# Forward token transforms in three rounded passes in place of one fp32 pass, in a two-layer GLA and Hyena encoder

## The reference, cut to what matters

```python
h = rmsnorm(x, norm_mix)
q, k, v, r, g_lr, hy_in = split(h @ w_in)
x = x + concat([gla_group(q, k, v, r, g_lr), hyena_group(hy_in)]) @ w_out
x = x + (silu(h2 @ w_gate) * (h2 @ w_up)) @ w_down        # h2 = rmsnorm(x, norm_ffn)

def fft_long_conv(u, k_freq, d):            # u: (B, 256, 512)
    y = irfft(rfft(u, n=512, axis=1) * k_freq, n=512, axis=1)[:, :256]
    return y + u * d

def hyena_group(u, ...):
    v, x1, x2 = split(short_conv_centred(u))
    k_freq = hyena_filters(...)             # sin-FFN(positions) @ w3, times exp(-t * deltas)
    z = x1 * fft_long_conv(v, k_freq[:, 0], skip[0])
    z = x2 * fft_long_conv(z, k_freq[:, 1], skip[1])
    return rmsnorm(z, norm_w)
```

## Time and profile before

| | us |
|---|---|
| median of 3 runs (lowest, highest) | 1272.35 (1271.86, 1273.59) |
| the profiled execution, device time | 1274.18 |
| its span in the profile | 1272.4 |
| TensorE busy | 1232.2 (97%) |
| VectorE busy | 712.2 (56%) |
| ScalarE busy | 683.5 (54%) |
| GpSimd busy | 674.1 (53%) |
| a unit's load of 512 KB, issue to landing, median | 3.5 |

### The profile page before, as it was taken

One profiled execution on the slowest core, in us unless ns is written; L12 is line 12 of the kernel. 1 busy time (PEld: TensorE's weight loads), 2 busy tenths in 40 slices (PEclk: granted clock), 3 DMA queues, 4 the chain that ended last, 5 costly groups with the idle time before them and its releaser, 6 DMA issues.

```text
span 1272.4 us, 23307 instructions
## 1 busy us (share of the span) xinstructions
PE 1232.2 (97%) x9196; PEld 1068.6 (84%) x9196; DVE 712.2 (56%) x1117; ACT 683.5 (54%) x1340; POOL 674.1 (53%) x483
## 2 busy tenths in 40 slices
PE   5989999999999999999999999999999999999997
PEld 4656877879999999988877777778899999998885
DVE  5865766667677777400057475674877776760003
ACT  5756664547665555422256765654576655653223
POOL 2565672566465354566636666428364433346661
PEclk9999999999999999999999999999999999999999
DMA  5211112140423323233322212123223323323222
GB/s 220 95 50 59 60 51 84 50 165 25 140 93 115 119 77 106 101 99 99 99 67 78 72 52 67 36 82 126 74 84 100 100 100 108 120 89 107 94 98 82
DMA packets 31211, 115.96 MB, mean 91 GB/s; under 512 B 3456, under 2 KB 3712, under 8 KB 30720
## 3 DMA queue, kind: packets, MB, share of 16 engines
q1 hardware_dynamic: 31104, 114.49, 26.6%
HBM read 112.37 MB, written 2.10 MB: 90 GB/s over the span
## 4 chain that ended last, share of the span: by engine, by line
PE 82%; DVE 8%; ACT 4%; issue 3%; POOL 1%; DMA 1%; SPq 0%; POOLq 0%; DVEq 0%; ACTq 0%
PE ps L1941 10%; PE ps L1944 10%; PE ps L1943 10%; PE ps L1805 6%; PE ps L1827 6%; PE ps L1825 6%; PE ps L1824 6%; PE ps L1807 6%; PE ps L1806 6%; PE ps L2084 2%; PE ps L2098 2%; PE ps L1821 2%; PE ps L1816 2%; PE ps L1818 2%; POOL w_lo L1141 1%
## 5 line engine op out<-in xcount | busy, mean ns | idle before, releaser
L1141 POOL TENSOR_TENSOR w_lo<-w_raw,w_hi 128x1024 fp32r<-128x1024 f32 x108 | 266.2, 2466 | 303.1 <-ACT w_hi L671 229.8
L671 ACT ACTIVATE w_hi<-w_raw 128x1024 fp32r<-128x1024 f32 x108 | 113.9, 1055 | 187.5 <-PE ps L1827 171.1
L1941 PE MATMUL ps<-h_hi,w_hi 128*128 128x256 f32 x672 | 191.0, 284 | 0.0
L1943 PE MATMUL ps<-h_lo,w_hi 128*128 128x256 f32 x672 | 190.1, 283 | 0.0
L1944 PE MATMUL ps<-h_hi,w_lo 128*128 128x256 f32 x672 | 190.1, 283 | 0.0
L1805 PE MATMUL ps<-h_hi,w_hi 128*128 128x512 f32 (+1 forms) x392 | 166.0, 423 | 3.8 <-POOL w_lo L1141 1.1
L1941 PE MATMUL ps<-sum_hi,w_hi 128*128 128x256 f32 x528 | 150.2, 284 | 3.6 <-DVE silu L1366 2.2
L1807 PE MATMUL ps<-h_hi,w_lo 128*128 128x512 f32 (+1 forms) x392 | 152.8, 390 | 0.0
L1806 PE MATMUL ps<-h_lo,w_hi 128*128 128x512 f32 (+1 forms) x392 | 152.2, 388 | 0.0
L1943 PE MATMUL ps<-sum_lo,w_hi 128*128 128x256 f32 x528 | 149.4, 283 | 0.0
L1944 PE MATMUL ps<-sum_hi,w_lo 128*128 128x256 f32 x528 | 149.3, 283 | 0.0
(11 more groups left out here) (269 smaller groups left out, 2824.7 us busy)
## 6 DMA issues: line engine op xcount, KB each, us to landing
w_raw<-in_units SPq DMA_DIRECT2D x110, 512.0 KB, 3.5
u<-in_pairs SPq DMA_DIRECT2D x44, 512.0 KB, 3.9
w_raw<-in_pairs SPq DMA_DIRECT2D x40, 512.0 KB, 4.0
gain<-in_gain SPq DMA_DIRECT2D x5, 512.0 KB, 4.3
par<-in_par SPq DMA_DIRECT2D x2, 1214.5 KB, 8.8
x<-in_x SPq DMA_DIRECT2D x4, 512.0 KB, 7.3
spec<-in_pairs SPq DMA_DIRECT2D x4, 512.0 KB, 5.0
out_y<-x SPq DMA_DIRECT2D x4, 512.0 KB, 2.6
```

The source lines that it names most:

```text
L671: nc.scalar.activation(w_tile(g, 0), w_raw[:, g % RAW], ACT.Copy).then_inc(s_hi, 1)
L1141: nc.gpsimd.tensor_tensor(w_tile(g, 1), w_raw[:, g % RAW], w_tile(g, 0).bitcast(F32), ALU.subtract).then_inc(s_lo, 1)
L1941: nc.tensor.matmul(out, hi[:, cols], factor[m][0][:, k], start=start and k == 0, stop=False, skip_group_check=True)
L1943: nc.tensor.matmul(out, hi[:, cols], factor[m][1][:, k], start=False, stop=False, skip_group_check=True)
```

## The change

Each token tile is now kept as `u_hi` (rounded by ACT) and `u_lo` (DVE, PSUM minus `u_hi`), and the table as `dft_hi` (ACT) and `dft_lo` (POOL). `spectrum` makes three `float32r` matmuls where there was one of float32. Everything that waited for `utc` before it used the tiles, or banks 6 and 7, now waits for `utl`, the count of the DVE subtractions. `dft_hi` and `dft_lo` stand where the decay window is, and `u_lo` where the last filter weights are, so the window is loaded anew once (512 KB) behind unit 29's load in layer 0, and DVE waits for that load before it makes the filters of layer 1.

```diff
-C_MISC = C_Z + P
+C_MISC = (C_Z + P + 7) // 8 * 8
@@ build: tiles
-        u_tok = sb("u_tok", 2 * HY, at=xs_at)[:, :].rearrange("p (t c) -> p t c", t=2)
+        u_hi = sb("u_hi", 2 * HY, F32R, at=xs_at)[:, :].rearrange("p (t c) -> p t c", t=2)
+        u_lo = sb("u_lo", 2 * HY, F32R, at=par_at + 4 * C_W3)[:, :].rearrange("p (t c) -> p t c", t=2)
+        dft_hi = sb("dft_hi", 4 * P, F32R, at=cst_at + 4 * K_WIN)[:, :].rearrange("p (f e c) -> p f e c", f=2, e=2)
+        dft_lo = sb("dft_lo", 4 * P, F32R, at=cst_at + 4 * K_WIN + 16 * P)[:, :].rearrange("p (f e c) -> p f e c", f=2, e=2)
@@ sync, behind load_unit
+                    if L + 1 < DEPTH and n == U_OUT + 4:
+                        sp.wait_ge(ufp.sem, ufp.at(L, 8))
+                        sp.dma_start(cst[:, K_WIN:N_CST], cst_d[:, K_WIN:N_CST]).then_inc(s_decay, 16)
@@ scalar, turn_copy
-                    nc.scalar.activation(u_tok[:, t], ps[:, 6 + t, :], ACT.Copy).then_inc(utc.sem, 1)
+                    nc.scalar.activation(u_hi[:, t], ps[:, 6 + t, :], ACT.Copy).then_inc(utc.sem, 1)
@@ scalar, slots, behind hi_unit and factors
+                    if slot == 9:
+
+                        act.wait_ge(abr.sem, abr.at(L, 4))
+                        nc.scalar.activation(dft_hi, dft, ACT.Copy).then_inc(s_dft_hi, 1)
@@ gpsimd, slots, behind lo_unit
+                    if slot == 9:
+                        pool.wait_ge(s_dft_hi, L + 1)
+                        nc.gpsimd.tensor_tensor(dft_lo, dft, dft_hi.bitcast(F32), ALU.subtract).then_inc(s_dft_lo, 1)
@@ vector
+            def token_rests(L, i):
+                for t in range(2):
+                    v.wait_ge(utc.sem, utc.at(L, 2 * i + t + 1))
+                    nc.vector.tensor_tensor(u_lo[:, t], ps[:, 6 + t, :], u_hi[:, t].bitcast(F32), ALU.subtract)\
+                        .then_inc(utl.sem, 1)
@@ vector, slots, near the start
+                    if (slot - 1, 1) in T_AT:
+                        token_rests(L, T_AT[slot - 1, 1])
                     if (slot - 1, 1) in D_AT:
                         spectrum_halves(L, D_AT[slot - 1, 1])
@@ vector, slots, near the end
+                    if (slot, 0) in T_AT:
+                        token_rests(L, T_AT[slot, 0])
                     if (slot, 0) in D_AT:
                         spectrum_halves(L, D_AT[slot, 0])
@@ vector, feed-forward of layer 0
                         if p == F_NET2 + 3:
                             hidden_pair(L + 1)
+                            v.wait_ge(s_decay, 16 * (L + 1))
@@ tensor, turn_v
                 if h == 3:
-                    pe.wait_ge(utc.sem, utc.at(L, 6))
+                    pe.wait_ge(utl.sem, utl.at(L, 6))
@@ tensor, spectrum
-                    pe.wait_ge(utc.sem, utc.at(L, 2 * i + 2))
+                    pe.wait_ge(utl.sem, utl.at(L, 2 * i + 2))
+                    if i == 0:
+                        pe.wait_ge(s_dft_lo, L + 1)
...
                 for f in range(2):
-                    last = nc.tensor.matmul(ps[:, 6 + f, :], dft[:, f, d], u_tok[:, d], start=True, stop=True)
+                    nc.tensor.matmul(ps[:, 6 + f, :], dft_hi[:, f, d], u_hi[:, d], start=True, stop=False)
+                    nc.tensor.matmul(ps[:, 6 + f, :], dft_hi[:, f, d], u_lo[:, d], start=False, stop=False)
+                    last = nc.tensor.matmul(ps[:, 6 + f, :], dft_lo[:, f, d], u_hi[:, d], start=False, stop=True)
@@ tensor, back, i < 3
-                    pe.wait_ge(utc.sem, utc.at(L, 2 * i + 4))
+                    pe.wait_ge(utl.sem, utl.at(L, 2 * i + 4))
```

More of the change, by code:

```diff
@@ L247, in build @@
         w_lo = sb("w_lo", RING * 1024, F32R)[:, :].rearrange("p (r c) -> p r c", r=RING)
+        cst_at = place[0]
         cst = sb("cst", N_CST)
         mask = sb("mask", len(MASKED) * NEAR, U8)[:, :].rearrange("p (l c) -> p l c", l=len(MASKED))
+        par_at = place[0]
         par = sb("par", N_PAR)
@@ L501, in build @@
         utc = Signal(sem("s_utc"), 8)
+        utl = Signal(sem("s_utl"), 8)
+        s_dft_hi, s_dft_lo, s_decay = sem("s_dft_hi"), sem("s_dft_lo"), sem("s_decay")
         ufp = Signal(sem("s_ufp"), 8)
```

## The result

| | before | after |
|---|---|---|
| median of 5 runs each, us (lowest, highest) | 1272.6 (1271.86, 1273.59) | 1282.65 (1281.98, 1283.47) |
| the profiled execution, device time | 1274.18 | 1282.65 |
| its span | 1272.4 | 1280.8 |
| TensorE busy | 1232.2 | 1231.2 |
| granted TensorE clock, mean over the span | 0.998 | 0.996 |

The changed kernel takes 1.0079 times as long, with an interval of 1.0064 to 1.0093: 10 us more, where 5.1 were forecast, and outside the range. The two spans differ by 8.4 only, since the profiled execution of before was 1.6 above its own median. (The granted clock of 0.998 before is the end of the program: from 1266.88 us on, 2.8 us behind the last matmul, the record shows 0.5. Every trace has such an end.) Further runs of the kernel before, made beside the experiments, give medians of 1272.5 to 1273.0.

A forecast was written before the change was run, and what follows sets the result against it. TensorE, busy 97% of the span, was taken as the bound. Per layer, new waits of 5.2 us against a gain of 2.7 give 5.1 us more in two layers: 1272.35 to 1277.4 us, range 1273.5 to 1280.5.

The forecast's parts named there:

- The bound: Whole kernel: TensorE, busy 97% of the span, sets the time; other engines cost only where TensorE waits for them.
- The gain: Token transforms: three float32r passes replace one float32 matmul, saving 0.33 us per call, 5.3 us over both layers.
- The waits: TensorE waits at slots 10, 13, 17 and 20; new parts 0.74, 1.17, 1.76 and 1.54, 5.2 us per layer.
- that rival: Slot 17: L1995 doesn't wait for head 2's reduction, so 1.76 us per layer falls away; 1273.9 us, chance 0.10.
- all is hidden: Rival: VectorE's subtractions fit in gaps at each place, so only the 5.3 us gain remains; 1267.0 us, chance 0.07.
- The covers: dft_hi, dft_lo and window reload lie beside other work, taken as nothing; subtractions not stretched by GpSimd, else 2.2 us more.
- the sum: Waits of 5.2 against gain of 2.7 us per layer, 5.1 more in two: median 1272.35 becomes 1277.4 us.
- one more cost: Rival: stretched subtractions (2.2 us) or one or two new TensorE stalls; 1279.6 us, chance 0.12.
- The stall of 1.10 in the earlier trace: TensorE at 777.98 in layer 1, cause unread; one or two such may come, or one may go, 1276.3 us.

The follow-up runs named there:

- e1_gain: Changed kernel without VectorE's subtractions, second pass reading u_hi in place of u_lo, TensorE waiting for ScalarE's copies: 1266.92 us, 0.9956 of the kernel before.
- e3_sum_first: Changed kernel with head 2's sum of squares ahead of spectrum_sums in slot 17 on VectorE: 1277.79 us, 1.0041 of the kernel before.
- e5_d_float: Changed kernel with round 3 of the token transforms left in float32, without rests: 1277.86 us, 1.0043 of the kernel before.
- e4_best: Changed kernel with slot 10's token copy ahead of queries, round 0's back mid-slot 13, o_sum first in slot 17, round 3 float32: 1271.47 us, ratio 0.9990.
- e2_cost: Changed kernel with subtractions and waits kept, but transforms in float32 of the rounded tile, rests unused: 1288.01 us, 1.0127 of the kernel before.
- e8_shift: Changed kernel with one 512-column float32 product in slot 1 of layer 0 made three times instead of once: 1283.16 us.
- e11_later8: Changed kernel with the first matmul of spectrum made eight times more in slot 10 of layer 0: 1285.68 us, 1.0097 of the kernel before.
- e6_two_rounds: Changed kernel with only rounds 0 and 2 rounded, slot 10's token copy ahead of queries, o_sum first in slot 17: 1269.60 us, ratio 0.9978 to before.
- e7_three_rounds: As the two-rounds kernel, but rounds 0, 1 and 2 rounded and back of round 0 at slot 13's start: 1270.43 us, 0.9983 of the kernel before.
- e9_back_first: As the kernel with all four waits taken away, but back ahead of level_step in the middle of slot 13: 1267.84 us, 0.9960 of the kernel before.

## Why the prediction was wrong, point by point

- **The bound** was right: every edit on another engine cost only where TensorE waited for it.
- **The gain** was right within 0.3 us, in part by luck: 5.3 forecast, 5.6 in `e1_gain`. The calls gave only 5.0 of it, 0.31 to 0.32 each instead of 0.33, here as in the changed kernel: the six steps of a call take 1.40 us, where six of 0.231 are 1.39, and the four steps before took 1.72. The other 0.6 is an old wait that went, and no part of the forecast. The rule of the Trainium skill (FP8 and Floating Point Precision, TensorE Precision Notes), true FP32 as four passes, would by the forecast's estimate have made the gain 7.4. `e1_gain` stands by the row, by which a float32 matmul costs 3.7 steps of a `float32r` one.
- **The waits** were right: forecast 0.74, 1.17, 2.1 and 2.0, measured 0.68, 1.08 to 1.12, 2.06 and 2.03. TensorE is 2.8 us later at the end of layer 0's slots than at their start, where 2.5 were forecast. `e3_sum_first` shows that L1995 waits for `osum`, so that rival fell; "all is hidden" fell with the four waits.
- **The covers** held. The subtractions stayed at 0.68, not 1.2 times as much. GpSimd was busy for the whole length of four of the 16 only, those of round 1; these took 0.676 to 0.679, the other 12 from 0.680 to 0.693. The rule of the Trainium skill (SBUF — State Buffer, Who interferes with whom) that a VectorE instruction with one SBUF input doesn't contend with GpSimd agrees with these four rows. `dft_hi`, `dft_lo` and the reload cost nothing that `e1_gain` could show.
- **The step that failed is the sum**, where it takes each wait at its length and every matmul behind it at 0.23. A wait of 2 us isn't over when TensorE starts again: behind two of the four, 3.41 us ran at half clock, for 1.43 and 1.62. The rival "one more cost" allowed 2.2 us for slower subtractions or for one or two stalls; it had neither this mechanism nor its size. The forecast had seen two waits of 2 us come into being where the old kernel had 0.3 and 0.5, and priced only their lengths. `e3_sum_first`, `e5_d_float` and `e4_best` show that the stretches go with the waits: four such waits have two stretches in the changed kernel, two have one in each of the next two kernels, and with none there is none. Which of the waits has one, nothing here forecasts.
- **The late row of VectorE**, 1.03 us, is in the five traces that have the rests of round 3 (after, `e2_cost`, `e3_sum_first`, `e8_shift`, `e11_later8`) and in none of those without them. That the rests cause it isn't shown, since a kernel without them also comes to this place earlier. From ScalarE's first copy in slot 10 to the first matmul of `xs` behind 280 us it takes 170.9 us or more in the five traces, and at most 170.4 in the others. The stall of 1.10 in the earlier trace rows, which might come or go, is in no other trace.
- **What is left.** The forecast is 5.25 us below the median. Half clock makes 3.05 of it, the late row 1.3 (its wait of 1.03 and what followed), the slots' 2.8 in place of 2.5 in each layer 0.6, and the base 0.25, since the median of five runs is 1272.6 and not 1272.35. That leaves 0.1. The profiled execution of before fits this only if it was 1.6 us slower than usual by its stall of 1.10 and a start that was 0.5 us later at slot 10 (117.89 against 117.37 for ScalarE's copy). Whether its other executions lack both isn't shown.

## What to carry to other kernels

Where an engine starts within 0.1 us of the one that it waits for, a low share of busy time hides nothing, and new work in that queue is paid in full; look also at what is queued behind it, as here a reduction of 0.69 us for another part of the kernel. Price a wait of TensorE of some 2 us at more than its length, since a stretch at half clock may follow it; in this kernel waits up to 1.77 us had none. Move what is waited for ahead of the new work, give the new work's reader something else to do first, and leave the change out where neither can be had (here round 3, for which nothing else was tried): that turned 10 us lost into 5 gained.

## What the runs showed of the hardware

- Behind a TensorE wait of 2.03 to 2.09 us the granted clock fell to 0.5 for 3.41 us in some places and not in others: behind 2 of 4 such waits in the changed kernel, 2 of 4 in the run of the costs alone, 1 of 2 with the reduction first, 1 of 2 with round 3 in float32, 2 of 4 in `e8_shift`, and 3 of 4 with eight more matmuls: 11 of 20. It began 0.3 to 1.8 us after the engine had started again, so never in the wait itself. The two of the changed kernel cost 1.43 and 1.62 us, a little less than half their length.
- In the traces with no wait of 2 us in slots 10 to 20 (the longest is 1.58) there was no such stretch there (before, `e1_gain`, `e4_best`, `e6_two_rounds`, `e7_three_rounds`, `e9_back_first`). Behind the longest wait of the earlier slots, 1.73 to 1.77 us at 71 to 73 us, there was none in any of twelve traces; the changed kernel's row:

```profile
71.86 1.55 PE L1988 MATMUL ps<-spec,cst 128*128 128x512 f32 x3 [1.76 <-DVE spec L1542]
```

- Which of these waits are followed by it differs from trace to trace, at the same places of the program. What decides it isn't shown.
- The granted clock is 0.5 also at the end of every program, 2 to 5 us behind the last matmul, and in `e9_back_first` from 15.81 to 22.64 us, behind a wait of 3.01 us.
- A row of VectorE took 1.76 to 1.77 us instead of 0.75 at one place, in each trace that has the rests of round 3. Whether they cause it isn't shown.
